# The per-layer embedding product of all rows is made ahead of the last stage's tiles and kept in on-chip memory

## What is computed

```
x = x + moe(rmsnorm(x, g_ffn))                                # top-4 of 32 experts
ple_gate = sigmoid(rmsnorm(x, g_ple) @ w_ple_gate)            # 1024 x 1024
x = x + ple_gate * (p @ w_ple)                                # p: 1024 x 256, w_ple: 256 x 1024
```

## Time and profile before

| what | value |
|---|---|
| time, median of 3 runs | 2656.31 us |
| time of the profiled execution | 2656.76 us |
| its span, first to last instruction | 2655.1 us |
| TensorE busy | 2521.5 us, 95% |
| VectorE busy | 898.5 us, 34% |
| ScalarE busy | 447.4 us, 17% |
| GpSimd busy | 349.6 us, 13% |
| mean granted clock of TensorE | 0.976 |

### The profile page before, as it was taken

One profiled execution on the slowest core, in us unless ns is written; L12 is line 12 of the kernel. 1 busy time (PEld: TensorE's weight loads), 2 busy tenths in 40 slices (PEclk: granted clock), 3 DMA queues, 4 the chain that ended last, 5 costly groups with the idle time before them and its releaser, 6 DMA issues. The chain is left out here.

```text
span 2655.1 us, 46713 instructions
## 1 busy us (share of the span) xinstructions
PE 2521.5 (95%) x16704; PEld 2080.9 (78%) x16704; DVE 898.5 (34%) x2591; ACT 447.4 (17%) x1066; POOL 349.6 (13%) x553
## 2 busy tenths in 40 slices
PE   8998889999989679999999999999999999999599
PEld 6755665444435379999999999999999999999344
DVE  4743665000013522223233332333333333333353
ACT  3323443000001101111111111111111111111132
POOL 2530000000002211001001011010101111110220
PEclk9998999999999889999999999999999999999799
DMA  4000002210045457677778778888888888885441
GB/s 145 17 17 9 1 0 61 75 47 24 24 148 121 123 205 289 243 272 288 278 273 298 267 286 321 288 297 290 310 308 310 313 307 321 298 329 211 166 168 71
DMA packets 273895, 518.81 MB, mean 195 GB/s; under 512 B 14849, under 2 KB 54417, under 8 KB 273842
## 3 DMA queue, kind: packets, MB, share of 16 engines
q1 hardware_dynamic: 236946, 445.55, 48.0%
q0 software_dynamic: 17600, 38.97, 4.3%
q10 hardware_dynamic: 19296, 33.56, 3.5%
HBM read 484.34 MB, written 33.70 MB: 195 GB/s over the span
## 5 line engine op out<-in xcount | busy, mean ns | idle before, releaser
L1527 PE MATMUL bank<-arena_a,arena_w 128*128 128x128 f32 (+4 forms) x8192 | 978.6, 282 | 1.1 <-DVE arena_a L1624 1.1
L1527 PEld LDWEIGHTS bank<-arena_a,arena_w 128*128 128x128 f32 x8192 | 971.9, 191 | 1.5 <-issue 1.5
L1536 PE MATMUL bank<-arena_a,arena_w 128*128 128x128 f32 (+4 forms) x4096 | 512.1, 282 | 0.0
L1536 PEld LDWEIGHTS bank<-arena_a,arena_w 128*128 128x128 f32 x4096 | 497.1, 191 | 0.0
L1646 DVE TENSOR_SCALAR arena_m<-bank,arena_m 128x160 f32<-128x160 f32 x256 | 98.2, 383 | 591.4 <-PE bank L1527 591.4
L1020 PE MATMUL bank<-arena_h,arena_w 128*128 128x512 f32 x448 | 194.5, 592 | 0.0
L1602 ACT ACTIVATE arena_m<-arena_m 128x160 f32<-128x160 f32 x256 | 82.8, 335 | 623.9 <-DVE arena_m L1646 623.6
L1657 DVE TENSOR_SCALAR arena_m<-bank,arena_m 128x32 f32<-128x32 f32 x256 | 64.1, 250 | 342.4 <-PE bank L1536 326.0
L1020 PEld LDWEIGHTS bank<-arena_h,arena_w 128*128 128x128 f32 x448 | 85.1, 190 | 107.2 <-issue 107.2
L1440 POOL DMA_DIRECT2D arena_m<-slot_tokens x33 | 19.0, 576 | 1109.7 <-issue 1103.5
L1608 ACT ACTIVATE arena_a<-bank 128x512 f32<-128x512 f32 x64 | 38.2, 597 | 597.7 <-PE bank L1572 597.7
(11 more groups left out here) (289 smaller groups left out, 2221.4 us busy)
## 6 DMA issues: line engine op xcount, KB each, us to landing
arena_w<-in_w_gate_up_dram SPq DMA_DIRECT2D x124, 2048.0 KB
arena_w<-in_w_down_dram SPq DMA_DIRECT2D x62, 2048.0 KB, 12.4
expert_rows<-arena_a ACTq DMA_DIRECT2D x32, 512.0 KB
arena_a<-in_x_dram SPq DMA_DIRECT2D x16, 512.0 KB, 3.4
arena_w<-in_w_in_dram SPq DMA_DIRECT2D x16, 512.0 KB, 5.4
arena_w<-in_w_gate_up_dram ACTq DMA_DIRECT2D x4, 2048.0 KB
arena_w<-in_w_o_dram SPq DMA_DIRECT2D x1, 4096.0 KB, 16.1
arena_w<-in_w_down_dram ACTq DMA_DIRECT2D x2, 2048.0 KB, 21.2
```

What stands on the lines that cost most here:

```text
L1527: m = pe.matmul(GU[f % 3][:, to:to + width], w[c][:, k, at:at + P], xT[:, k, 0:width], start=(k == 0), stop=(k == K - 1), skip_group_check ...
L1536: return pe.matmul(DN[d % 2][:, 0:width], wd[d // CT][:, k, at:at + P], actT[:, k, 0:width], start=(k == 0), stop=(k == KF - 1), skip_grou ...
```

## The change

The embedding product of all eight tiles is computed ahead of the tiles' loop, and its result (1024 x 1024, 4 MB) is kept in `arena_a`.

- In `experts`, SyncE loads all of p (1 MB) into `arena_m` beside the weights of the last stage. Behind the last item, TensorE turns p by 16 transposes into four banks, ScalarE copies two of them and VectorE two into `pT`, and TensorE makes the product of tiles 4 and 5 (`embed`); ScalarE copies each from its pair of banks to `emb` (`keep_embedding`). ScalarE's part stands behind its last stores and ahead of its wait for them.
- In `combine`, TensorE makes the products of tiles 6, 7, 0, 1 and 2 first of all, and that of tile 3 behind the transposes of tile 0; two pairs of banks take turns. ScalarE copies the first five ahead of the norm of tile 0 and the sixth behind its copy of the turned tile 0.
- In the loop over the tiles the loads of p, the two transposes of p, their copy and the embedding product are gone. VectorE multiplies the sigmoid by the kept tile in one instruction of 128x1024 instead of two of 128x512. The sigmoids of a tile now wait in every tile for VectorE's output row of the tile before (`out`), and the first product of VectorE waits for all 16 copies (`emb_kept`).

```diff
--- before.py
+++ after.py
@@ -1447,6 +1447,26 @@
             pool.indirect_dma_start(xq, None, h2_quarters, bass.IndirectOffsetOnAxis(idx_q, 0)).then_inc(rows_here, 16)
             wait_value(pool, rows_here, 32 * i + 32)
 
+        EMB_EARLY, EMB_LATE = (4, 5), (6, 7, 0, 1, 2, 3)
+        w_emb = view(arena_m, 4096, KP, D)
+        p_rows = view(arena_m, 6144, T, PLE)
+        pT = view(arena_w, 22 * D, KP, S)
+        emb = view(arena_a, 0, T, D)
+        emb_kept = top.enter_context(nc.semaphore("emb_kept"))
+
+        def embed(pe, n, pair, done):
+
+            for j, bank in enumerate(pair):
+                for k in range(KP):
+                    m = pe.matmul(bank[:, :], pT[:, k, n * P:(n + 1) * P], w_emb[:, k, j * BANK:(j + 1) * BANK],
+                                  start=(k == 0), stop=(k == KP - 1))
+            m.then_inc(done, 1)
+
+        def keep_embedding(act, n, pair):
+
+            for j, bank in enumerate(pair):
+                act.activation(emb[:, n, j * BANK:(j + 1) * BANK], bank[:, :], ACT.Copy).then_inc(emb_kept, 1)
+
         def experts():
             ctx, sem = stage("ex")
             with ctx:
@@ -1461,6 +1481,15 @@
                 yR = view(arena_m, 12 * WIDTH + K * P, K, REST)
                 GU, TX, DN, YA, YB = banks[0:3], banks[3], banks[4:6], banks[6], banks[7]
                 x_rest, x_bank = YB, (TX, YA)
+                p_bank = (TX, GU[0], GU[1], GU[2])
+                emb_banks = ((DN[0], DN[1]), (GU[0], GU[1]))
+
+                def keep_p(eng, q):
+
+                    into = pT[:, q // 2, (q % 2) * BANK:(q % 2 + 1) * BANK]
+                    if q % 2:
+                        return eng.tensor_copy(into, p_bank[q][:, :])
+                    return eng.activation(into, p_bank[q][:, :], ACT.Copy)
 
...
                         sp.dma_start(view(arena_h, 0, K, D), w_ple_gate.rearrange("(k p) n -> p k n", p=P)).then_inc(sem("ple"), 16)
-                        sp.dma_start(view(arena_m, 4096, KP, D), w_ple.rearrange("(k p) n -> p k n", p=P)).then_inc(sem("ple"), 16)
+                        sp.dma_start(w_emb, w_ple.rearrange("(k p) n -> p k n", p=P)).then_inc(sem("ple"), 16)
+                        sp.dma_start(p_rows, p2d.rearrange("(t p) n -> p t n", p=P)).then_inc(sem("ple"), 16)
                         sp.dma_start(gain_row[:, :], g_ple[0].partition_broadcast(P)).then_inc(sem("ple"), 16)
...
-                        sp.wait_ge(sem("ple"), 48)
+                        sp.wait_ge(sem("ple"), 64)
 
                     @block.gpsimd
                     def _(pool):
@@ -1585,6 +1615,19 @@
                                 item(i, width)
                         turn_y(K * n, K - 1, True)
 
+                        pe.wait_ge(sem("ple"), 64)
+                        wait_value(pe, sem("xT_act"), 2 * n + 2)
+                        wait_value(pe, sem("gu_read"), KF * n)
+                        for q, bank in enumerate(p_bank):
+                            for j in range(4):
+                                t, k = 4 * (q % 2) + j, q // 2
+                                m = pe.transpose(bank[:, j * P:(j + 1) * P], p_rows[:, t, k * P:(k + 1) * P], ident[:, :])
+                            m.then_inc(sem("p_psum"), 1)
+                        pe.wait_ge(sem("pT_act"), 2)
+                        pe.wait_ge(sem("pT_dve"), 2)
+                        for n_emb, pair in zip(EMB_EARLY, emb_banks):
+                            embed(pe, n_emb, pair, sem("emb_psum"))
+
                     @block.scalar
                     def _(act):
                         def keep_x(i):
@@ -1614,6 +1657,12 @@
                             for h in (0, 1):
                                 to = y_dram[bass.ds(row + P, REST), h * BANK:(h + 1) * BANK]
                                 act.dma_start(to.rearrange("r (j c) -> j r c", c=P), y_b[:, h, :]).then_inc(sem("stored"), 16)
+                        for q in (0, 2):
+                            act.wait_ge(sem("p_psum"), q + 1)
+                            keep_p(act, q).then_inc(sem("pT_act"), 1)
+                        for j, (n_emb, pair) in enumerate(zip(EMB_EARLY, emb_banks)):
+                            act.wait_ge(sem("emb_psum"), j + 1)
+                            keep_embedding(act, n_emb, pair)
                         wait_value(act, sem("stored"), 48 * n + 48)
 
                     @block.vector
...
+                        for q in (1, 3):
+                            dve.wait_ge(sem("p_psum"), q + 1)
+                            keep_p(dve, q).then_inc(sem("pT_dve"), 1)
...
         def combine():
             ctx, sem = stage("comb")
             with ctx:
                 w_gate = view(arena_h, 0, K, D)
-                w_emb = view(arena_m, 4096, KP, D)
                 yg = [[view(arena_w, D * (4 * b + j), D) for j in range(TOP_K)] for b in (0, 1)]
                 x1, x2, xn, outt = ([view(arena_w, D * (8 + 2 * j + b), D) for b in (0, 1)] for j in range(4))
                 xnT = [view(arena_w, D * (16 + b), K, P) for b in (0, 1)]
-                pt = [view(arena_m, 6144 + PLE * b, PLE) for b in (0, 1)]
-                pT = [view(arena_m, 6144 + PLE * (2 + b), KP, P) for b in (0, 1)]
...
-                TB0, TB1, TP = banks[0:3]
-                gate_bank, emb_bank = banks[4:6], banks[6:8]
+                TB0, TB1 = banks[0:2]
+                gate_bank = banks[4:6]
+                emb_banks = (banks[6:8], banks[2:4])
                 with nc.Block() as block:
                     @block.sync
...
-                            sp.dma_start(pt[b], p2d[b * P:(b + 1) * P, :]).then_inc(sem(f"x{b}"), 16)
...
-                                sp.dma_start(pt[b], p2d[rows, :]).then_inc(sem(f"x{b}"), 16)
...
@@ -1721,7 +1769,7 @@
                     @block.vector
                     def _(dve):
                         def norm(n, b):
-                            wait_value(dve, sem(f"x{b}"), 16 * n + (32 - 16 * b))
+                            wait_value(dve, sem(f"x{b}"), 8 * n + (16 - 8 * b))
                             wait_value(dve, sem(f"y{b}"), 32 * n + (64 - 32 * b))
                             for j in range(TOP_K):
                                 last = j == TOP_K - 1
@@ -1742,12 +1790,11 @@
 
                         def finish(n, b):
                             wait_value(dve, sem("sig"), 2 * n + 2)
-                            wait_value(dve, sem("emb_psum"), n + 1)
+                            if isinstance(n, int) and n == 0:
+                                dve.wait_ge(emb_kept, 2 * T)
                             wait_value(dve, sem("rows_free"), n + 1)
-                            for j in (0, 1):
-                                half = slice(j * BANK, (j + 1) * BANK)
-                                dve.tensor_tensor(outt[b][:, half], emb_bank[j][:, :], sig[:, half], ALU.mult).then_inc(sem("gated"), 1)
-                            wait_value(dve, sem("gated"), 2 * n + 2)
+                            dve.tensor_tensor(outt[b], emb[:, bass.ds(n, 1), :].rearrange("p o d -> p (o d)"), sig, ALU.mult).then_inc(sem("gated"), 1)
+                            wait_value(dve, sem("gated"), n + 1)
                             dve.tensor_tensor(outt[b], outt[b], x2[b], ALU.add).then_inc(sem("out"), 1)
                             wait_value(dve, sem("out"), n + 1)
 
@@ -1767,34 +1814,45 @@
                         def keep(n, b):
                             wait_value(act, sem("xnT_psum"), n + 1)
                             act.activation(xnT[b][:, 0:4, :].rearrange("p k t -> p (k t)"), TB0[:, :], ACT.Copy).then_inc(sem("xnT"), 1)
-                            act.activation(pT[b].rearrange("p k t -> p (k t)"), TP[:, 0:KP * P], ACT.Copy).then_inc(sem("xnT"), 1)
 
                         def gate(n, b):
                             wait_value(act, sem("gate_psum"), n + 1)
-                            if isinstance(n, int) and n == T - 1:
-                                act.wait_ge(sem("out"), T - 1)
+                            if not (isinstance(n, int) and n == 0):
+                                wait_value(act, sem("out"), n)
                             for j in (0, 1):
                                 act.activation(sig[:, j * BANK:(j + 1) * BANK], gate_bank[j][:, :], ACT.Sigmoid).then_inc(sem("sig"), 1)
 
+                        def late_embedding(j):
+                            act.wait_ge(sem("emb_psum"), j + 1)
+                            keep_embedding(act, EMB_LATE[j], emb_banks[j % 2])
+
                         def ready(n, b):
+                            if isinstance(n, int) and n == 0:
+                                for j in range(len(EMB_LATE) - 1):
+                                    late_embedding(j)
                             norm(n, b)
                             keep(n, b)
+                            if isinstance(n, int) and n == 0:
+                                late_embedding(len(EMB_LATE) - 1)
                         ahead_loop(act, T, ready, nothing, gate)
 
```

(27 more changed lines are left out.)

## The result

Six runs of the changed kernel have a median of 2668.96 us (2666.35 to 2674.9), six of the kernel before 2655.56; the ratio is 1.0055 with a 95% interval of 1.0043 to 1.0068. It is slower: by 13.4 us between the medians, by 14.6 by the ratio; 2668.7 us was forecast, 12.4 above the kernel before. The profiled execution took 2668.48 us, its span is 2666.9.

A forecast was written before the change was run, and what follows sets the result against it. TensorE alone was taken to bound the steady tiles, 18.58 us each. Terms 6.7 + 0.85 + 2.3 + 1.05 - 4.6 - 2.4 = +3.9, plus 8.5 for five clock falls, gave +12.4: 2668.7 us, range 2657 to 2677.

The forecast's parts named there:

- last tile: After gate product 7: VectorE begins at 2647.26 instead of 2649.61, behind the sigmoids; 2.4 us gained.
- Part 1: Steady tiles: sigmoids are late next, so only 0.66 of 3.66 us is gained per tile, 4.6 us over seven.
- Part 3: Behind the last expert item: the stage change waits for the added products and copies; 6.7 us lost, plus 0.85 for clock.
- The clock term: Ahead of the two products behind the last expert item: idle TensorE may lose full clock; 0.85, half of 1.7 us.
- Part 4: First tiles of the last stage: square waits for the fifth copy, 2.3 us lost; slow start after idling, 1.05 lost.
- Part 5: Idle gaps of 3.08 us before seven gate products lower TensorE's clock; five falls of 1.7 us, 8.5 us lost.
- the clock holds in gaps of 3.1 us: Rival on the gaps before seven gate products: no clock falls, sum 3.05 us, time 2659.4 us; chance 0.2.
- the early part costs nothing: Rival at the expert stage's end: the change waits for stores, not TensorE and ScalarE; 7.6 us off, 2661.1; chance 0.08.
- transposes don't keep the clock: Rival on steady tiles: 3.95 us without counted work, all seven fall, 1.7 to 2.6 us each; 2672.1 to 2678.7; chance 0.22.
- The forecast: Main case for the gaps before gate products: three to six clock falls, 2664 to 2671 us; chance 0.5.
- the third rival: Steady tiles: transposes do not keep the clock, all seven gate products fall, 2672.1 to 2678.7 us; chance 0.22.
- the second: Rival at the expert stage's end: early part costs nothing; 2661.1 us, or 2652.7 with the clock held; chance 0.08.

The follow-up runs named there:

- e3: Kernel before, with the embedding product made for tile 0 only, 24 us of matmuls less: 1.0025 of the kernel before.
- e4: Changed kernel plus one-column spare sigmoids and roots on ScalarE, so both table loads lie where it is idle: 0.9983 of the kernel before.
- e7: Kernel before plus the same one-column spare sigmoids and roots as e4: 0.9988 of the kernel before.
- e2: Changed kernel without the two embedding products behind the last expert item and their copies: 1.0023 of the kernel before.
- e5: Changed kernel with the norm of tile 0 ahead of ScalarE's copy of the fifth product: 1.0036 of the kernel before.
- e1: Changed kernel plus three unread 128x512 matmuls behind the transposes of tiles 1 to 7, filling TensorE's gap: 1.0017 of the kernel before.
- e10: As e1 on the changed kernel, but one matmul instead of three, leaving about 2.4 us idle: 1.0050 of the kernel before.
- e9: As e1 on the changed kernel, but 24 transposes of 128x128 in place of the matmuls: 1.0021 of the kernel before.
- e6: e4 plus two pairs of banks for gate products of even and odd tiles: 0.9956 of the kernel before.
- e8: e6 with only tile 4's product behind the last item, left in banks; six products before the first transpose; tile 0's norm before the fifth copy: 0.9911, median 2632.74 us.

## Why the prediction was right

Step by step, on the two profiled executions (us, plus is slower):

| step | forecast | measured | from |
|---|---|---|---|
| end of the expert stage | +6.7, clock +0.85 | +8.8 | 6.37 became 15.13 |
| stage start to first transpose | +2.3 | +2.4 | 20.43 became 22.82 |
| first transpose to end of gate product 0 | +1.05 | +0.2 | 20.35 became 20.52 |
| seven distances between gate products | -4.6 | -3.9 | mean 4.66 became 4.10 |
| slow gate products | +8.5 (five) | +8.5 (five of 1.7) | 13.97 or 15.67 |
| last tile | -2.4 | -2.4 | 3.52 became 1.15 |
| sum | +12.4 | +13.6 | |

In the profiled execution of the changed kernel the expert stage ended 1.7 us earlier (2466.82 against 2468.51), in work that the change doesn't touch, so the spans differ by 11.8 only. The forecast met the median (2668.7 against 2668.96) closer than its terms deserve, and that is luck: the terms that changed come to 1.2 us more than forecast, and the six runs of the kernel before now have a median 0.75 us below the one it started from.

- **Part 1, the sigmoids are late next.** Right, and shown by e3 and e4: of 3.66 us taken from TensorE per tile 0.56 came back. The gap was sized 3.08 and measured 3.23; the mis-sized term is mainly the release of the gate product behind the sigmoids, 0.14 us instead of 0.05; the other 0.06 are rows a few hundredths longer ahead of it. I had read 0.05 off a wait for a copy. For the same reason I took the gate product of the kernel before to be held by the embedding product, where it was held by the sigmoids by a hair (e7). VectorE's loop didn't bind, as argued (ahead of tile 4 its scaling ended at 2582.30, 0.57 us before gate product 3 did). The table load had no drain behind it: in the chain of the changed kernel the sigmoids start 0.01 behind the load's end (2526.82 + 1.28, then 2528.11), and the drain of 1.38 us that the Trainium skill adds to a switch (ScalarE: Activation LUTs, "What ACT_TABLE_LOAD costs") is not there on this path.
- **Part 3, the stage change waits.** Right (e2): 8.7 us for two products. The clock term was sized too small: the idle 2.97 us ahead of the two products did lower it, and they took 8.83 us, 1.95 over the 6.88 at full clock, where half of 1.7 had been put in.
- **Part 4.** The wait of the square for the fifth copy is as worked out (e5: one changed order brings the first transpose 3.0 sooner). The start behind the 5.4 us of idle time cost 2.1 us (20.52 against 18.4) instead of 3.0.
- **Part 5, the clock.** Shown by e1: with the gap filled all of it vanishes. That five of seven fell was a guess between 0 and 7 that came out exactly in the profiled execution, and in e2 and e10 too; e5 had four, e3 six of six. The hit is luck. How many fall in the runs that weren't profiled is open: the changed kernel's six spread over 8.5 us, but e1's eleven, with the gaps filled, spread over 8.0, so the spread says nothing of it.
- **The rivals.** That the clock holds in gaps of 3.1 us fell with the first trace, and e10 has as many falls behind 2.38. That the early part costs nothing fell with e2. That transposes don't keep the clock fell with e9: the granted clock was 1.00 over all seven filled gaps. The Trainium skill's statement that a transpose does not count as busy the same way (TensorE: Matmul & The Clock Gate, "Part 4: PE-mode transpose") does not agree with these traces.
- **The chances.** The forecast and the third rival, 0.72, with half of the second are 0.76; the prediction has 0.74 for slower. Nothing hangs on it.

So the change moved 29 us of TensorE work (3.66 in each of eight tiles) off the steady path, and got back 3.9 + 2.4 = 6.3, since ScalarE's chain lay right beneath it. It paid 8.8 and 2.4 for where the work went, and 8.5 for the idle time that it left behind. What it does bring is room: with the product kept, the load can leave the gap (e4), a second pair of gate banks is free (e6), and the products fit where TensorE idled (e8), 0.9% faster than before.

## What to carry to other kernels

Before work is taken off the busiest engine, ask what lies beneath it on the others: the gain is the distance to the next one, here 0.56 of 3.66 us. Idle time on TensorE can have a second price: here 1.7 us behind most gaps of 2.4 to 3.5 us, nothing behind those of 1.8. So a removal has to keep the gap that it opens short, and hiding the wait beneath (here by loading ScalarE's tables early) must go with it. Work put behind a stage's last item was hidden only where it ended before the stage would have ended anyway, as the single product of e8 did and the two of the change did not; a result can wait in its banks across the stage change.

## What the runs showed of the hardware

- Gaps of 1.8 us never lowered the granted clock (seven in e4), those of 2.4 did in five of seven (e10), of 3.2 in five of seven (the changed kernel, e2) or four of seven (e5), of 3.51 in six of six (e3). One fall costs 1.7 us of a gate product (15.67 against 13.97).
- Transposes (24 of them, 2.78 us, in each of seven gaps) kept the granted clock at 1.00 (e9).
- An activation of one column, 0.20 us, moves a table load of 1.28 us to where it is hidden (e4).
